# First pair's products in five steps inside the modulation, token loads and stores moved to GpSimd's queue, zeroing of result rows over 16 rows

## The chip, the cores and the metric

The kernel runs on one core of one Trainium2 chip. The metric is the device time of one execution in microseconds (us), and a kernel's time is the median over its runs. The engines are TensorE (PE; its weight loads are PEld), VectorE (DVE), ScalarE (ACT) and GpSimd (POOL). SyncE (SP) computes nothing and issues transfers; SPq, ACTq and POOLq stand for the instruction streams that issue transfers.

## The reference

A two-layer diffusion backbone works on 1024 latent tokens and 256 context tokens of width 1024. Layer 0 is neighbourhood attention with 16 heads and a hierarchical mixture of experts, layer 1 a bidirectional recurrent block and another mixture of experts. All layers are modulated by rows made from the condition vectors:

```python
m = silu(cond) @ ada_w[l] + ada_b[l]       # 6 * 1024 values, for c and for c_ctx
h = rmsnorm(x, norm_g[l, 0]) * (1 + scale) + shift
qkv = h @ w_qkv + b_qkv                    # one pair of heads: 128 columns each of q, k, v
s = softmax(q k^T / 8 + bias)              # window of 8 x 16 positions and all context keys
x = x + gate * ((s v) @ w_o + b_o)
y = sum over 2 chosen experts of weight * (silu(h w1[e]) * (h w3[e])) @ w2[e]
```

The first three lines are the modulation stage here; attention follows. The experts write their result rows to a buffer in DRAM, which must be zero where no expert writes, so that a later gather reads zeros.

## The kernel before, in words

**modulation** (L170 to L458) is one block of five instruction streams. The two condition vectors are multiplied by `ada_w`, 50.3 MB in all. It is read in NG = 6 groups g of 2048 columns, each in KD = 8 tiles k of 128 x 2048 (1 MB), so 48 tiles in 8 buffers. For each tile TensorE does four products of 512 columns ("ada product", L431). The profile counts each as two passes, so one tile is x8. At a group's end DVE adds the bias `ab` and writes `mo[g % 2]` (L388, four adds), and ACT stores `mo` to `mod_d` (L311) and loads the bias rows of group g + 2 (L269). A tile may be loaded again once the group before has used its buffer (`a_used`, L219).

Group 0 holds shift and scale for the first norm. After it TensorE spreads them over 128 partitions (L445), DVE makes `g_rows` (L393) and ACT `sh_rows` (L300). From then on the ten token tiles n (128 tokens each, eight of `x` and two of `ctx`) are prepared beside the groups:

- load into `xt[n % 4]` by SP (L208). From n = 4 on SP waits in its queue until tile n - 4 is normed (`h_ok`, L207)
- sum of squares on DVE (`squares`, L326), square root on ACT (`root_`, L259), then reciprocal, scale and shift on DVE (`norm`, L334 to L340) into `hb[n % 3]`
- eight transposes on TensorE (L456) into PSUM, and copy to `hT` by ACT (`evac`, L263).

`WITH` says which tiles are normed after which group: 0, 1, 2 after group 0; 3, 4, 5 after group 1; 6, 7 after group 2; 8, 9 after group 3. Their transposes stand at the start of the next group. ACT's stream is strictly in order: pieces of the group, the wait for `m_ready`, bias loads, store, the `evac`s, the `root_`s.

Two token tiles make a chunk c of 256 tokens. `FIRST` places the q, k and v products of the first pair of heads for each chunk (`piece`, L406 and L271) behind ada products: V at (g, k), K at (g, k + 1), T (two transposes of V) and Q at (g, k + 2), with the five places (2,0), (3,0), (3,3), (4,0), (5,0). V, K and Q are eight matmuls of 256 columns each (x16 in the profile, L420), T is L413. `LOAD_X` and `LOAD_SLAB` say behind which ada tile SP loads tokens and the three weight slabs.

**attention** (L505 to L778) starts when every stream of modulation has ended. Per pair h of 8, TensorE does the scores, transposes and outputs of pair h and between them the products of pair h + 1 (L726), V first. SP loads the slabs of pair h + 1 (L550) and the bias tables (L555), and zeroes an eighth of the result rows, 592 rows of 4 KB, in one transfer (`clear_slots`, L558 to L562). The source is `zero`, and the rows are laid out over 74 partitions, 8 rows from each. In SP's queue the first of these transfers stands in front of the slabs of pair 1. The block ends only when all eight have landed (L570).

```python
        load_pair(0, first=True)
        sp.wait_ge(zr_ok, 1)
        clear_slots(0)
        with sp.Fori(1, PAIRS) as h:
            load_pair(h)
            clear_slots(h)
        sp.wait_ge(cl_ok, 16 * PAIRS)
```

Everything after attention (projection, experts, combine, recurrent layer) is untouched.

Of the kernel before, what the change touches and what calls it, by code (L numbers as in the profile page):

```python
# [11 lines left out]
ACT = mybir.ActivationFunctionType  # L12
# [74 lines left out]
def program(nc, A, out):  # L87
    root = ExitStack()
    with root:
# [51 lines left out]
        def by_columns(rows_ap, n):  # L141
# [28 lines left out]
        def modulation(hT, first, room):  # L170
            slab, qT, kT, VT, V, bq, mask, sl_in, w_ps, w_used = first
            with ExitStack() as st:
# [14 lines left out]
                ss, rt = sbuf(st, "ss_b", [P, 2]), sbuf(st, "rt_b", [P, 2])  # L187
                c_in, c_th, c_si, a_ch = sem("c_in"), sem("c_th"), sem("c_si"), sem("a_ch")
                ab_in, bq_in, bq_ok = [sem(f"ab_in{j}") for j in range(2)], sem("bq_in"), sem("bq_ok")
                w_in = [sem(f"ada_in{k}") for k in range(KD)]  # L190
                a_used = sem("ada_used")
                m_ready, m_out = sem("mod_ready"), [sem(f"mod_out{j}") for j in range(2)]
                k_id, k_done, k_io, k_cst = sem("k_id"), sem("k_done"), sem("k_io"), sem("k_cst")
                ng_in, rows_ps, gain_ok, sh_ok = sem("b_ng"), sem("b_rows"), sem("b_gain"), sem("b_shift")
                x_in = [sem(f"b_x{j}") for j in range(NXB)]
# [5 lines left out]
                with nc.Block() as block:  # L201
                    @block.sync
                    def _(sp):
                        def load_x(n):
                            src = by_columns(A["x"][0], n) if n < NTL else A["ctx"][0, (n - NTL) * P:(n - NTL + 1) * P, :]
                            if n >= NXB:
                                sp.wait_ge(h_ok, n - NXB + 1)  # L207
                            sp.dma_start(xt[n % NXB][:, :], src).then_inc(x_in[n % NXB], 16)  # L208
# [4 lines left out]
                        for n in range(FRONT):  # L213
                            load_x(n)
# [11 lines left out]
                        sp.wait_ge(bq_in, 16)  # L226
# [24 lines left out]

                    @block.scalar
                    def _(a):
                        def root_(n):
                            j = n % 2
                            a.wait_ge(sum_ok, n + 1)
                            if n >= 2:
                                a.wait_ge(dv, 2 * (n - 2) + 1)
                            a.activation(rt[:, j:j + 1], ss[:, j:j + 1], ACT.Sqrt, bias=epst[:, :]).then_inc(sqrt_ok, 1)  # L259
# [5 lines left out]

                        def load_bias(g):
                            for j in range(QT):
                                for r in range(2):
                                    a.dma_start(ab[32 * j + r:32 * j + r + 1, g % 2, :], abv[j, :, g]).then_inc(ab_in[g % 2], 16)  # L269
# [16 lines left out]
                        load_bias(0)  # L286
                        load_bias(1)
# [8 lines left out]
                        for g in range(NG):  # L296
                            if g == 0:
                                for w, part, b0 in ROWS_PS[1::2]:
                                    a.wait_ge(rows_ps, 2 * w + 2)
                                    a.activation(sh_rows[:, w, :], banks(b0, 2), ACT.Copy).then_inc(sh_ok, 1)  # L300
                            for i, (pg, k, what, c) in enumerate(FIRST):
                                if pg == g:
                                    piece(i, what, c)
                            for n in WITH.get(g - 1, ()):
                                if n in LATE:
                                    root_(n)
                            a.wait_ge(m_ready, QT * (g + 1))
                            if g + 2 < NG:
                                load_bias(g + 2)
                            for j in range(QT):  # L310
                                a.dma_start(mod_d[:, g * GC + j * CW4:g * GC + (j + 1) * CW4],  # L311
                                            mo[g % 2][32 * j:32 * j + 2, :]).then_inc(m_out[g % 2], 16)
                            for n in WITH.get(g - 1, ()):
                                evac(n)
                            for n in WITH.get(g, ()):
                                if n not in LATE:
                                    root_(n)
                        for b in range(2):
                            a.wait_ge(m_out[b], 16 * QT * NG // 2)

                    @block.vector
                    def _(v):
                        def squares(n):
                            j = n % 2
                            v.wait_ge(x_in[n % NXB], 16 * (n // NXB) + 16)
                            v.tensor_tensor_reduce(junk, xt[n % NXB][:, :], xt[n % NXB][:, :], 1.0 / D, 0.0, ALU.mult, ALU.add,  # L326
                                                   ss[:, j:j + 1]).then_inc(sum_ok, 1)
                            v.wait_ge(sum_ok, n + 1)

                        def norm(n, w):  # L330
                            j, b = n % 2, n % NHB
                            link = Chain(v, dv, 2, n)
                            v.wait_ge(sqrt_ok, n + 1)
                            link(v.reciprocal(ss[:, j:j + 1], rt[:, j:j + 1]))  # L334
                            if n >= NHB:
                                v.wait_ge(tr_ok, n - NHB + 1)
                            link(v.scalar_tensor_tensor(out=hb[b][:, :], in0=xt[n % NXB][:, :], scalar=ss[:, j:j + 1],
# [40 lines left out]
                        for n in range(3):  # L378
                            once(v.tensor_copy(tile(1, n), expand(rowp[:, :], (2, GC_))))
                            once(v.tensor_tensor(tile(0, n), tile(1, n), expand(colp[:, n * GC_:(n + 1) * GC_], (1, GR)), ALU.max))  # L380
                        for g in range(NG):
                            v.wait_ge(a_used, KD * (g + 1))
                            v.wait_ge(ab_in[g % 2], 16 * 2 * QT * (g // 2 + 1))
# [12 lines left out]
                            tiles = WITH.get(g, ())  # L396
                            for n in tiles:
                                if n == tiles[0] or n in LATE:
                                    squares(n)
                                if n != tiles[-1] and n + 1 not in LATE:  # L400
                                    squares(n + 1)
                                norm(n, 0 if n < NTL else 1)

                    @block.tensor
                    def _(t):
# [17 lines left out]

                        t.wait_ge(c_si, 1)
                        for g in range(NG):
                            if g >= 2:
                                t.wait_ge(m_ready, QT * (g - 1))
                            for k in range(KD):
# [19 lines left out]
                            for n in WITH.get(g - 1, ()):  # L448
                                t.wait_ge(h_ok, n + 1)
                                if n >= 2:  # L450
                                    t.wait_ge(ev_ok, n - 1)
                                else:
                                    t.wait_ge(sh_ok, 2)
                                    t.wait_ge(gain_ok, 2)
                                for k in range(KD):
# [1398 lines left out]
```

## Time and profile before

| what | value |
|---|---|
| time, median of 3 runs | 3108.96 us (3108.54 to 3112.82) |
| the profiled execution's own time | 3110.24 us |
| span of its trace | 3108.4 us |
| granted clock of TensorE, mean | 0.921 of full speed |
| modulation block | 0 to 198.6 us |
| attention block | 198.6 to 925.8 us |
| busy PE / DVE / ACT / POOL | 85% / 35% / 30% / 13% |

The profiled execution lies 1.84 us outside of its span and 1.28 us above the median. A timeline row gives the start, the duration, the engine, the line of the kernel, the operation, output and inputs, the number of instructions merged, and in brackets the idle time before with what ended it. The clock is the share of full speed that was granted to TensorE.

### The profile page before, as it was taken

Reading aid. Unit: us, or ns where it says so; the run is one execution under the profiler, and the core shown is the slowest. Engines: PE = TensorE matmul, PEld = TensorE weight load, DVE = VectorE, ACT = ScalarE, POOL = GpSimd, SP = SyncE. Lnnn points to the kernel's source line nnn. Section 1 sums busy time; section 2 is a strip of 40 time slices with the busy share of each in tenths; the row PEclk is TensorE's granted clock in tenths of the full one; section 3 lists DMA queues with packets and bytes.
Section 4 is the critical chain, followed back from the end, with each engine's and each line's share of the span. In section 5 each row is a group of like instructions: output and inputs, shape, how many; then the busy total and the mean of one; then the engine's idle time right before and its main releaser. Section 6 shows DMA issues by size and latency. Waiting matters only on the chain. (4 is left out here: it accounts for less than half of the span.)

```text
span 3108.4 us, 68456 instructions
## 1 busy us (share of the span) xinstructions
PE 2628.8 (85%) x27112; PEld 1751.6 (56%) x27113; DVE 1092.4 (35%) x2328; ACT 927.1 (30%) x2036; POOL 389.8 (13%) x574
## 2 busy tenths in 40 slices
PE   5857999999978959999999359999959599999980
PEld 1536777777754536666666224544425466666650
DVE  3312333333343342222222564556444322222226
ACT  1113444344440003333333223334310033333332
POOL 0000000000001102222222310000011022222223
PEclk8878999999998979999999669999979699999995
DMA  9832111111105347999999550010042589999986
GB/s 352 301 120 74 58 46 46 51 40 58 44 26 160 102 192 300 416 411 406 417 417 417 209 150 27 27 40 27 0 165 88 216 354 413 405 417 417 418 343 225
DMA packets 157785, 652.37 MB, mean 210 GB/s; under 512 B 41600, under 2 KB 55936, under 8 KB 102368
## 3 DMA queue, kind: packets, MB, share of 16 engines
q1 hardware_dynamic: 126512, 547.79, 45.3%
q10 hardware_dynamic: 15600, 55.79, 4.6%
q0 software_dynamic: 15552, 47.20, 4.2%
q8 instruction: 73, 1.20, 0.2%
q14 instruction: 48, 0.39, 0.0%
HBM read 575.65 MB, written 75.07 MB: 209 GB/s over the span
## 5 line engine op out<-in xcount | busy, mean ns | idle before, releaser
L1155 PE MATMUL PS<-wt,xT 128*32 128x256 f32 x13056 | 753.2, 381 | 56.4 <-issue 28.3
L1155 PEld LDWEIGHTS PS<-wt,xT 128*32 128x32 f32 x13056 | 505.2, 110 | 274.4 <-issue 80.3
L726 PE MATMUL PS<-hT,slab 128*128 128x256 f32 x1680 | 386.1, 383 | 39.0 <-DMA slab<-in_qkv_s 38.5
L1095 ACT ACTIVATE y<-PS 32x256 f32<-32x256 f32 x832 | 311.6, 375 | 304.1 <-PE PS L1170 295.3
L1170 PE MATMUL PS<-wt,hidT 128*32 128x256 f32 x6528 | 396.1, 380 | 3.5 <-ACT y L1095 3.5
L726 PEld LDWEIGHTS PS<-hT,slab 128*128 128x128 f32 x1680 | 312.7, 191 | 84.6 <-DMA slab<-in_qkv_s 38.9
L1308 DVE STREAM_TRANSPOSE xT<-xg 128x256 f32<-128x256 f32 x210 | 93.5, 445 | 706.8 <-PE PS L1155 686.5
L1170 PEld LDWEIGHTS PS<-wt,hidT 128*32 128x32 f32 x6528 | 256.6, 110 | 100.9 <-issue 5.6
L1060 POOL DMA_INDIRECT xg<-h_d,ib x216 | 211.3, 978 | 174.8 <-POOL ib L1057 174.8
L1089 ACT ACTIVATE th<-PS 128x128 f32<-128x128 f32 x210 | 58.3, 277 | 526.2 <-PE PS L1155 521.0
L661 DVE TENSOR_REDUCE low<-PS 128x1 f32<-128x256 f32 x160 | 66.2, 422 | 415.1 <-PE PS L707 344.0
L1750 PE MATMUL PS<-uT,wg 128*128 128x512 f32 (+1 forms) x384 | 148.0, 545 | 20.5 <-ACT tr L1577 20.5
L933 PE MATMUL PS<-wo,OT 128*128 128x512 f32 x320 | 143.9, 609 | 17.7 <-DMA wr<-in_moe_w_expert 9.2
L1739 PE MATMUL PS<-hT,wu 128*128 128x512 f32 (+1 forms) x384 | 140.0, 526 | 8.1 <-DMA wu<-in_lru_w_in 8.1
L1057 POOL COPY ib<-idx 128x1 int32 (+1 forms) x216 | 39.3, 182 | 850.0 <-DVE xT L1308 707.1
L835 POOL TENSOR_TENSOR xt_p<-xt_p,bg 128x1024 f32<-128x1024 f32 x18 | 42.1, 2343 | 827.2 <-DVE bg L850 658.9
L933 PE MATMUL PS<-wo,zT 128*128 128x512 f32 x256 | 115.3, 610 | 35.2 <-DMA wo<-in_lru_w_o 29.1
L629 ACT ACTIVATE probT<-PS 128x640 f32<-128x640 f32 (+2 forms) x160 | 98.7, 617 | 110.0 <-PE PS L736 108.4
L1750 PEld LDWEIGHTS PS<-uT,wg 128*128 128x128 f32 x384 | 75.7, 198 | 94.9 <-issue 70.2
L736 PE MATMUL PS<-ident,prob 128*128 128x128 f32 x672 | 106.7, 284 | 21.6 <-issue 10.2
L1320 DVE STREAM_TRANSPOSE hidT<-hid 128x128 f32<-128x128 f32 x208 | 64.8, 312 | 169.8 <-PE PS L1170 168.7
L620 ACT ACTIVATE prob<-PS,low 128x640 f32<-128x640 f32 (+2 forms) x160 | 112.9, 708 | 25.0 <-DVE low L670 23.1
(248 smaller groups left out, 2588.1 us busy)
## 6 DMA issues: line engine op xcount, KB each, us to landing
wt<-in_w SPq DMA_DIRECT2D x256, 1024.0 KB, 22.8
wt<-in_w2s SPq DMA_DIRECT2D x128, 1024.0 KB, 23.2
OT<-in_ada_w SPq DMA_DIRECT2D x30, 1024.0 KB, 18.6
ys_d<-y ACTq DMA_DIRECT2D x52, 512.0 KB, 7.8
ys_d<-zero SPq DMA_DIRECT2D x8, 2368.0 KB
aw<-in_ada_w SPq DMA_DIRECT2D x18, 1024.0 KB, 23.1
slab<-in_qkv_s SPq DMA_DIRECT2D x24, 512.0 KB, 3.8
x_d<-x_p ACTq DMA_DIRECT2D x18, 512.0 KB, 3.4
```

What stands on the lines that cost most here:

```text
L620: a.activation(prob[j][:, 0:n], SF[:, o:o + n], ACT.Exp, bias=bias, scale=-1.0, accum_out=sums[:, j:j + 1]).then_inc(ex_ok, 1)
L629: a.activation(probT[j][:, 0:n], PT[:, 0:n], ACT.Copy).then_inc(pe_ok, 1)
L726: mm = pe.matmul(W, slab[m][:, k, :], hT[:, k, c * PIECE:(c + 1) * PIECE], start=(k == 0), stop=(k == KD - 1))
L736: mm = pe.transpose(PT[:, c * P:(c + 1) * P], prob[j][:, c * P:(c + 1) * P], ident[:, :])
L933: mm = t.matmul(PS[:, 2 * (n % 2) + h, :], Z[:, k, n * P:(n + 1) * P], wo[:, k, h * 512:(h + 1) * 512], start=(k == 0), stop=(k == KD - 1))
L1060: g.indirect_dma_start(out=xg[j][:, :], out_offset=None, in_=h2v, in_offset=bass.IndirectOffsetOnAxis(ap=ib[j][:, :], axis=0)).then_inc(g_ ...
L1095: ins = a.activation(buf[STRIP * j:STRIP * (j + 1), g * QD:(g + 1) * QD], PS[32 * g:32 * g + 32, DOWN, 0:QD], ACT.Copy)
L1155: mm = t.matmul(PS[32 * g:32 * g + 32, UP, 0:QD], xT[:, k * 32:k * 32 + 32], wt[b][:, q, c * 1024 + g * QD:c * 1024 + g * QD + QD], start= ...
L1170: mm = t.matmul(PS[32 * g:32 * g + 32, DOWN, 0:QD], hT[:, k * 32:k * 32 + 32], wt[b][:, q, c * 1024 + g * QD:c * 1024 + g * QD + QD], star ...
L1308: v.transpose(xT[:, :], xg[j][:, :]).then_inc(xT_ok, 1)
L1739: mm = t.matmul(dst[:, c:c + wd], w[:, k, o * P:(o + 1) * P], hT[:, k, c:c + wd], start=(k == 0), stop=(k == KD - 1))
L1750: mm = t.matmul(dst[:, c:c + wd], wg[:, q, k, o * P:(o + 1) * P], uT[k][:, c:c + wd], start=(k == 0), stop=(k == 1))
```

## The change

The transposes of chunk c now stand behind one ada product of their own (`STEPS`: (1,4), (2,3), (3,2), (4,1), (5,0)), and the chunk's V, K, T and Q behind the next three, so a step comes every seven tiles. `AFTER` says which chunks DVE norms after which group. The sums and roots have ten columns instead of two, tiles 0 and 1 have their squares taken before group 0 is done, and ACT takes the roots of tiles n + 2 ahead of the copies of n. SP loads only tokens 0 to 3; tokens 4 to 9, all bias rows (one transfer for both rows instead of two) and the stores of `mo` are issued by GpSimd. `clear_slots` uses 16 partitions with 37 rows from each, and slot 0 is cleared last.

```diff
-        WITH, LATE = {0: (0, 1, 2), 1: (3, 4, 5), 2: (6, 7), 3: (8, 9)}, (4, 5)
-        NHB, NXB, FRONT = 3, 4, 3
-        LOAD_X = {(1, 0): 3, (2, 3): 4, (2, 4): 5, (2, 6): 6, (2, 7): 7, (3, 5): 8, (3, 7): 9}
-        LOAD_SLAB = {(1, 2): 2, (1, 4): 1, (1, 6): 0}
-        FIRST = [(g, k + i, what, c) for c, (g, k) in enumerate(((2, 0), (3, 0), (3, 3), (4, 0), (5, 0)))
-                 for what, i in (("V", 0), ("K", 1), ("T", 2), ("Q", 2))]
+        AFTER = {0: (0, 1), 1: (2,), 2: (3,), 3: (4,)}
+        STEPS = ((1, 4), (2, 3), (3, 2), (4, 1), (5, 0))
+        FIRST = [(g, k + i, what, c) for c, (g, k) in enumerate(STEPS)
+                 for what, i in (("V", 1), ("K", 2), ("T", 3), ("Q", 3))]
+        NHB, NXB = 3, 4
+        LOAD_X, LOAD_SLAB = {(1, 0): 2, (1, 1): 3}, {(1, 2): 2, (1, 3): 1, (1, 4): 0}
...
-                        for n in range(FRONT):
-                            load_x(n)
+                        load_x(0)
+                        load_x(1)
...
+                        def load_bias(n):
+                            for j in range(QT):
+                                row = abv[j, 0, n, :]
+                                both = bass.AP(tensor=row.tensor, offset=row.offset, ap=[[0, 2], [1, CW4]])
+                                g.dma_start(ab[32 * j:32 * j + 2, n % 2, :], both).then_inc(ab_in[n % 2], 16)
+
+                        def store(n):
+                            g.wait_ge(m_ready, QT * (n + 1))
+                            for j in range(QT):
+                                g.dma_start(mod_d[:, n * GC + j * CW4:n * GC + (j + 1) * CW4],
+                                            mo[n % 2][32 * j:32 * j + 2, :]).then_inc(m_out[n % 2], 16)
+
+                        def load_x(n):
+                            src = by_columns(A["x"][0], n) if n < NTL else A["ctx"][0, (n - NTL) * P:(n - NTL + 1) * P, :]
+                            g.wait_ge(h_ok, n - NXB + 1)
+                            g.dma_start(xt[n % NXB][:, :], src).then_inc(x_in2[n % NXB], 16)
+
+                        load_bias(0)
+                        load_bias(1)
+                        for n in range(NG):
+                            store(n)
+                            if n + 2 < NG:
+                                load_bias(n + 2)
+                            for c in AFTER.get(n, ()):
+                                for x in (2 * c + NXB, 2 * c + NXB + 1):
+                                    if x < NT:
+                                        load_x(x)
+                        for b in range(2):
+                            g.wait_ge(m_out[b], 16 * QT * NG // 2)
...
+                        root_(0)
+                        root_(1)
+                        for w, part, b0 in ROWS_PS[1::2]:
+                            a.wait_ge(rows_ps, 2 * w + 2)
+                            a.activation(sh_rows[:, w, :], banks(b0, 2), ACT.Copy).then_inc(sh_ok, 1)
+                        for c in range(NT // 2):
+                            for n in (2 * c, 2 * c + 1):
+                                if n + 2 < NT:
+                                    root_(n + 2)
+                            for n in (2 * c, 2 * c + 1):
+                                evac(n)
+                            for i, (_, _, what, pc) in enumerate(FIRST):
+                                if pc == c:
                                     piece(i, what, c)
...
+                        squares(0)
+                        squares(1)
                         for g in range(NG):
...
-                            tiles = WITH.get(g, ())
-                            for n in tiles:
-                                if n == tiles[0] or n in LATE:
-                                    squares(n)
-                                if n != tiles[-1] and n + 1 not in LATE:
-                                    squares(n + 1)
-                                norm(n, 0 if n < NTL else 1)
+                            for c in AFTER.get(g, ()):
+                                for n in (2 * c, 2 * c + 1):
+                                    if c:
+                                        squares(n)
+                                for n in (2 * c, 2 * c + 1):
+                                    norm(n, 0 if n < NTL else 1)
...
+                                if (g, k) in STEPS:
+                                    for n in range(2):
+                                        turn(2 * STEPS.index((g, k)) + n)
...
-                            n, rows = SLOTS // PAIRS, 74
+                            n, rows = SLOTS // PAIRS, 16
                             dst = ys_d[bass.ds(h * n, n), :].rearrange("(i p) d -> p i d", p=rows)
                             sp.dma_start(dst, expand(zero[0:rows, :], (1, n // rows))).then_inc(cl_ok, 16)
 
                         load_pair(0, first=True)
                         sp.wait_ge(zr_ok, 1)
-                        clear_slots(0)
                         with sp.Fori(1, PAIRS) as h:
                             load_pair(h)
                             clear_slots(h)
+                        clear_slots(0)
                         sp.wait_ge(cl_ok, 16 * PAIRS)
```

`turn(n)` is the former loop of eight transposes with its waits, made a function.

## Rows read from the trace of the kernel before

**Rows 1.** Costliest groups on the page: the products of the next pairs on PE
```profile
L726 PE MATMUL PS<-hT,slab 128*128 128x256 f32 x1680 | 386.1, 383 | 39.0 <-DMA slab<-in_qkv_s 38.5
```
**Rows 2.** Busy time of stretches of early attention; the first row names the columns
```profile
core 0: us, PE busy (x) PEld busy (x) DVE busy (x) ACT busy (x) POOL busy (x), PEclk, DMA share, GB/s
...
210.90:249.40 38.50, 0.00 (x0) 0.00 (x1) 2.63 (x9) 2.25 (x5) 0.00 (x0) 0.50 0.27 97
249.40:292.00 42.60, 42.60 (x268) 33.92 (x270) 13.44 (x40) 17.02 (x37) 3.86 (x4) 0.95 0.13 54
```
**Rows 3.** Timeline of early attention: SP's issues, and PE on both sides of its gap
```profile
199.57 0.34 SPq L562 DMA_DIRECT2D ys_d<-zero  x1
...
200.82 36.68 SPq L550 DMA_DIRECT2D slab<-in_qkv_s  x3
...
209.74 1.12 PE L736 MATMUL PS<-ident,prob 128*128 128x128 f32 x4
...
249.40 5.75 PE L726 MATMUL PS<-hT,slab 128*128 128x256 f32 x16 [38.54 <-DMA slab<-in_qkv_s]
```
**Rows 4.** DMA: rate over 0 to 250 us in 6.25 us slices; issues from 198 to 212
```profile
GB/s 108 261 399 422 420 324 420 414 417 417 357 266 325 246 263 424 415 415 419 274 287 275 218 48 275 270 421 121 0 3 69 51 52 52 53 53 230 140 50 53
...
ys_d<-zero SPq DMA_DIRECT2D x1, 2368.0 KB
slab<-in_qkv_s SPq DMA_DIRECT2D x1, 512.0 KB, 48.5
```
**Rows 5.** What SP's queue waited for from 62 to 93 us: total, times, longest
```profile
SPq L208 <- DVE hb_b L340: 13.4, 2, 12.9
SPq L220 <- PE PS L431: 12.9, 6, 4.5
```
**Rows 6.** Timeline: PE's ada products at tiles (0,0), (1,0) to (1,3), and (1,7)
```profile
16.76 1.89 PE L431 MATMUL PS<-OT,csil 128*2 128x512 f32 x8 [16.76 <-DMA OT<-in_ada_w]
...
44.20 5.84 PE L431 MATMUL PS<-OT,csil 128*2 128x512 f32 x32
...
61.57 1.89 PE L431 MATMUL PS<-aw,csil 128*2 128x512 f32 x8 [1.85 <-DMA aw<-in_ada_w]
```
**Rows 7.** Timeline of group 4: transposes, squares, copies to hT, pieces V, K, Q, ada products
```profile
137.98 1.97 PE L456 MATMUL PS<-ident,hb_b 128*128 128x128 f32 x16
...
142.25 1.22 DVE L326 CUSTOM_DVE_ANT_0 gt_rows<-xt_b 128x1024 f32<-128x1024 f32 x1
...
144.68 1.94 ACT L263 ACTIVATE hT<-PS 128x1024 f32<-128x1024 f32 x2 [7.95 <-issue]
...
146.76 5.85 PE L420 MATMUL PS<-hT,slab 128*128 128x256 f32 x16 [5.85 <-ACT hT L263]
...
153.52 3.72 PE L420 MATMUL PS<-hT,slab 128*128 128x256 f32 x16
...
158.41 3.62 PE L420 MATMUL PS<-hT,slab 128*128 128x256 f32 x16
...
163.68 2.76 PE L431 MATMUL PS<-aw,csil 128*2 128x512 f32 x24
```
**Rows 8.** Timeline: end of modulation
```profile
193.10 2.84 DVE L388 TENSOR_TENSOR mo<-PS,ab 2x512 f32<-2x512 f32 x4 [23.75 <-PE PS L431]
195.97 1.16 ACTq L311 DMA_DIRECT2D mod_d<-mo  x4
...
198.59 0.96 POOL L574 MEMSET zero<- 128x1024 f32 x1 [195.19 <-POOLq L201]
```
**Rows 9.** Transfers issued by GpSimd: one in the first expert stage; the gathers, us to landing
```profile
1160.05 0.98 POOL L1060 DMA_INDIRECT xg<-h_d,ib  x1 [0.83 <-POOL ib L1057]
...
y_c<-ys_d,ib_c POOLq DMA_INDIRECT x36, 6.5
```
**Rows 10.** Timeline: last zeroing transfer, last computing instruction of attention
```profile
793.23 0.28 SPq L562 DMA_DIRECT2D ys_d<-zero  x1
...
925.30 0.28 ACT L638 ACTIVATE OT<-PS 128x128 f32<-128x128 f32 x1 [0.84 <-PE PS L759]
```

More of the change, by code:

```diff
@@ L186, in modulation @@
                 hb = [sbuf(st, f"hb_b{j}", [P, D]) for j in range(NHB)]
[L187 removed]
+                ss, rt = sbuf(st, "ss_b", [P, NT]), sbuf(st, "rt_b", [P, NT])
                 c_in, c_th, c_si, a_ch = sem("c_in"), sem("c_th"), sem("c_si"), sem("a_ch")
[L189 removed]
+                ab_in, bq_in, bq_ok = [gather_sem(f"ab_in{j}") for j in range(2)], sem("bq_in"), sem("bq_ok")
                 w_in = [sem(f"ada_in{k}") for k in range(KD)]
                 a_used = sem("ada_used")
[L192 removed]
+                m_ready, m_out = sem("mod_ready"), [gather_sem(f"mod_out{j}") for j in range(2)]
                 k_id, k_done, k_io, k_cst = sem("k_id"), sem("k_done"), sem("k_io"), sem("k_cst")
                 ng_in, rows_ps, gain_ok, sh_ok = sem("b_ng"), sem("b_rows"), sem("b_gain"), sem("b_shift")
[L195 removed]
+                x_in, x_in2 = [sem(f"b_x{j}") for j in range(NXB)], [gather_sem(f"b_more{j}") for j in range(NXB)]
                 sum_ok, sqrt_ok, h_ok, tr_ok, ev_ok = sem("b_sum"), sem("b_sqrt"), sem("b_h"), sem("b_tr"), sem("b_ev")
@@ L254, in root_ @@
                         def root_(n):
-                            j = n % 2
                             a.wait_ge(sum_ok, n + 1)
-                            if n >= 2:
-                                a.wait_ge(dv, 2 * (n - 2) + 1)
-                            a.activation(rt[:, j:j + 1], ss[:, j:j + 1], ACT.Sqrt, bias=epst[:, :]).then_inc(sqrt_ok, 1)
+                            a.activation(rt[:, n:n + 1], ss[:, n:n + 1], ACT.Sqrt, bias=epst[:, :]).then_inc(sqrt_ok, 1)
                         def evac(n):
@@ L295, in _ @@
                         a.wait_ge(k_id, 3)
[L296 to L302, printed above, removed]
-                                    piece(i, what, c)
[L304 to L319, printed above, removed]
+                        root_(0)
[11 more added lines that the diff above has]
+                                if pc == c:
+                                    piece(i, what, c)
                     @block.vector
@@ L422, in piece, with turn @@
                             mm.then_inc(w_ps, 1)
+                        def turn(n):
+                            t.wait_ge(h_ok, n + 1)
+                            if n >= 2:
+                                t.wait_ge(ev_ok, n - 1)
+                            else:
+                                t.wait_ge(sh_ok, 2)
+                                t.wait_ge(gain_ok, 2)
+                            for k in range(KD):
+                                mm = t.transpose(banks(2 + 2 * (n % 2), 2)[:, k * P:(k + 1) * P],
+                                                 hb[n % NHB][:, k * P:(k + 1) * P], ident[:, :])
+                            mm.then_inc(tr_ok, 1)
                         t.wait_ge(c_si, 1)
@@ L447, in _ @@
                                     mm.then_inc(rows_ps, 1)
[L448 to L455, printed above, removed]
-                                    mm = t.transpose(banks(2 + 2 * (n % 2), 2)[:, k * P:(k + 1) * P],
-                                                     hb[n % NHB][:, k * P:(k + 1) * P], ident[:, :])
-                                mm.then_inc(tr_ok, 1)
         def load_rows(eng, s, l, sub, ng_row, tmp_ng):
```

29 lines of the change are left out of this document (11 added, 18 removed).

## The prediction, made before the changed kernel was run

> **What bounds the kernel now.** I read the costliest groups first and looked for idle time of TensorE, the busiest engine. One row stands out: the products of the next head pair sat idle 39.0 us, of which 38.5 wait for a weight slab [rows 1]. The stretches say that this is one hole: from 210.9 to 249.4 PE does nothing at a clock of 0.50, and behind it PE is busy all of the time [rows 2]. So a gap closed in early attention should be gained in full.
>
> The timeline gives the cause. SP issued the zeroing of slot 0 at 199.57 and the slabs only then, its three slab issues stretching over 36.68 us; PE stopped after 209.74 + 1.12 = 210.86 and went on at 249.40 [rows 3]. While the zeroing ran the core moved 51 to 53 GB/s, where loads over 128 partitions ran at 415 to 422; the first slab took 48.5 us to land [rows 4]. 53/420 is an eighth, two engines of 16: 2.42 MB / 53 = 45.7 us, so the zeroing ended at about 246 and the slab's share behind it on those two a little later. The part of the Trainium skill on this (DMA: Bandwidth & Descriptors, "Why a DMA increments its semaphore by 16 and not by 1") says that a DMA uses the largest number up to 16 that divides the slowest dimension of both sides; that makes 2 of 74, as the rate shows, and 16 of 16.
>
> The second place is modulation, 198.6 us. Its DMA runs at 420 GB/s up to 62 us, then at 246 to 357 in four of the next five slices, and falls again after 119 [rows 4]. SP's queue shows why in the first of these: it stood 12.9 us at one token load that waits for a norm, with ada tiles queued behind [rows 5]. Near the middle PE works, but each group has a hole: in group 4 the V piece waited 5.85 us for the copies to `hT`, because ACT does the store of `mo` first, and then ran at 5.85 instead of 3.72 us, at the lower clock [rows 7].
>
> **The slab wait.** Clearing slot 0 goes behind everything, so slab V of pair 1 is the first large transfer of attention. It is issued at about the place of the old zeroing, 12.3 us after the block's start PE wants it, and three slabs are 1.57 MB, 3.7 us at 420. It has landed long before. Removed: 249.40 - 210.86 = 38.5 us. The first piece behind the gap was cold (5.75 us [rows 3]) and will be, since PE is cold in the first 12 us anyway; nothing for that. Bounds: 36, if another operand is late next (bias tables, whose loads are behind the slabs), and 40, if the clock rises sooner. I take 38.5.
>
> **Zeroing on 16 partitions.** Seven transfers come one per pair, behind that pair's slabs, and two at the end. No row has a transfer of 16 partitions. Between the full rate (2.42 MB / 420 = 5.8 us) and that of 74 partitions (45.7) the time is the same: the last issue was at 793.23, attention ended at 925.6 [rows 10], 132 us for two transfers of at most 45.7. Cost 0 at either; PE's work hides it.
>
> **Modulation, up to the first step.** Two instead of three token tiles stand ahead of `ada_w`: 0.52 MB / 420 = 1.25 us, so tile (0,0) lands at 15.5 instead of 16.76, and group 1 starts on PE at 42.95 instead of 44.20 [rows 6]. Bias loads leave ACT for GpSimd, hidden behind the tiles of group 0. Before, tile (1,7) was there at 61.57 [rows 6]. SP's list up to it holds as many bytes as before with those two tiles counted, but GpSimd may issue tokens 4 to 7 from about 46 us on, as norms end, which share the 16 engines: up to 4 x 1.25 = 5 us, so it lands between 61.6 and 66.6. Chunk 0 runs in the same time: transposes at about 53, then V (cold, 5.85), K and Q. That ends near 72, no longer at the start of group 2 behind all copies and stores. Four ada products later, at 75 to 80, step 1 begins; I take 76. PE's queue had the same transposes at 63 but its products from 74 to 88.
>
> **Modulation, step by step.** From step 1 on all seven tiles of a step cost, warm: two transposes 1.97; product and V 0.9 + 3.65; product and K the same; product, T and Q 1.2 + 3.65 (153.52 + 3.72 to 158.41 is 1.2); four more products at 2.76/3 = 0.92, 3.7 [rows 7]. Sum 19.6, and 0.4 for the end of the second copy: 20 us. DMA needs 7 x 2.5 = 17.5, plus 2.5 for two tokens in one step, so PE sets the pace and no tile is late. Steps 1 to 4 and the rest: 4 x 20 = 80 us.
>
> New waits: `root_(n + 2)` stands ahead of the copies on ACT, and its sum comes after the group's adds on DVE. Step 2 is at (3,2): from the end of (2,7) it takes adds 2.84, two sums 2.6, a root 0.3, two copies 1.94 [rows 7, 8], with handovers 8.1 us, while PE has 3 products, the transposes and one product, 5.5: late by 2.6. Step 3 at (4,1) has one product less: 3.5. Steps 1 and 4 have room or no roots. After such a pause V may be cold, as in [rows 7]: 2 us each. Together 10 us (bounds 0 and 12). PE then ends at 76 + 80 + 10 = 166 (158 to 176).
>
> **The end of the block.** Before: adds from 193.10 to 195.94, attention's first instruction at 198.59 [rows 8], 2.65 later. GpSimd now issues the four stores. The only rows of its issues are gathers, 0.98 each and 0.83 idle between [rows 9], against 1.16 us for ACT's four. Four are 3.9 to 7.2, so 2.8 to 6.0 more, below by 0 if small ones are cheap; I take 2.8, as the stores compute no indices. End: 166 + 0.1 + 2.84 + 2.65 + 2.8 = 174.4, that is 24.2 less than 198.6. Ends: 158 + 5.6 = 163.6 (35 gained) and 176 + 5.6 + 6 = 187.6 (11).
>
> **Sum.** 38.5 + 24.2 = 62.7 us; from the profiled 3110.24 this gives 3047.5, from the median, 1.28 lower, 3046.3. All behind attention moves forward unchanged. Nothing within 0.2% (6.2 us) can be told from no change here.
>
> **Rivals.**
> - *Modulation gains almost nothing* (0 to 11 us). The work of SP's queue waits in POOL's instead; every step waits for DVE or ACT, and PE falls cold each time (5 steps x 5 us are the 25). For it: the roots ahead of the copies. Against it: only two steps have less room than the chain needs. Time 3108.96 - 38.5 - 6 = 3065 (3059 to 3071). In the Trainium skill (Trainium Kernel Development and Optimization, "Key Constraints") DMAs of all three queues share the same engines, and using several of them only saves issue time. By that the token loads gain nothing, and the time is this rival's. But SP's 12.9 us [rows 5] are a wait inside the queue, no issue time. Chance 0.13.
> - *The stalls don't come* and modulation follows its transfers: over 35 us gained, 3034 or less. Against it the DVE chain above. Chance 0.05.
> - *The 16 rows go over fewer engines.* Two change nothing. One would make 91 us of each: issued at 793.23, the last two would end at 976, 50 us after attention's old end of 925.6 [rows 10], and slabs queued behind would wait some 2 us per pair, 12 together: 3046 + 62 = 3108, no change. Below 37 GB/s it begins to cost. The quotient 53/420 for 74 speaks for a rule of divisors, so against it. Chance 0.02.
> - *GpSimd's queue becomes the bound* (slower). After the adds of group 0 at 38.6 it has 24 stores, 16 bias loads and 6 token loads, 46 in a strict order, and DVE waits for bias and stores of two groups earlier. At t us each the block ends at 38.6 + 46 t + 2: 0.98 [rows 9] gives nothing, and it decides from 2.9 us on, where it passes 174. Slower than before, 38.5 us being gained in attention, needs t over 4.3. If each transfer waited for the one before to land, 6.5 us as the gathers take [rows 9], the block would end at 340: 3109 + 141 - 38.5 = 3212. Against it: gathers follow each other at 1.8 us, not 6.5. Chance 0.03.
>
> **How the numbers follow.** Forecast 0.75 (3036 to 3059), rivals 0.13, 0.05, 0.02, 0.03; 0.02 for what I don't see. The bounds of the terms give 3108.96 - 36 - 11 = 3062 and 3108.96 - 40 - 35 = 3034; they hold the forecast's case and a third of the first rival, about 0.8. Faster by over 0.2%: 0.95; within: 0.02; slower: 0.03.
>
> **What would show it.** No wait of PE for a slab in early attention, and in the 50 us after its start full-rate slices, then slices of zeroing at a high rate, not at 53. Modulation ends at 174 (164 to 188). SP waits only for ada buffers. PE's V pieces of steps 2 and 3 wait 2 to 4 us for ACT's copies, the others under 1. Four POOL issues of about 1 us follow the last adds. I am wrong if the gap before L726 merely moves to another operand, if the steps are further apart than 24 us, or if stages behind attention change in length.

## The result and the profile after

The changed kernel takes 3093.45 us (3090.72 to 3098.35, 5 runs) against 3110.51 for the kernel before in the same comparison: a ratio of 0.9947 with the interval 0.9932 to 0.9961. It is 17 us faster where 62.7 were predicted, and lies outside the predicted range. Its profiled execution has a span of 3089.5 us, 18.9 less than before. By blocks:

| block | before | after | change | predicted |
|---|---|---|---|---|
| modulation | 198.6 | 183.6 | -15.0 | -24.2 |
| attention | 727.2 | 719.1 | -8.1 | -38.5 |
| all behind it | 2182.6 | 2186.8 | +4.2 | 0 |

Each kernel has one trace, and blocks with the same code differ from trace to trace. Modulation as before takes 192.5 to 198.6 us (the kernel before and runs 3 and 4), the changed one 181.8 to 186.2 us (the changed kernel and runs 1, 2 and 5 to 8). So the gain there is 15.0 us in this pair of traces, and 6 to 17 us if other pairs are taken. One source of the spread is the clock of single V pieces: the last one took 6.54 us in the kernel before and 3.69 in runs 3 and 4.

From the changed kernel's page, the row that answers to [rows 1] and two others that grew:

```profile
L741 PE MATMUL PS<-hT,slab 128*128 128x256 f32 x1680 | 387.9, 384 | 0.5
...
L751 PE MATMUL PS<-ident,prob 128*128 128x128 f32 x672 | 106.9, 285 | 47.6 <-ACT probT L644 28.2
...
L644 ACT ACTIVATE probT<-PS 128x640 f32<-128x640 f32 (+2 forms) x160 | 98.7, 617 | 139.5 <-PE PS L751 97.0
```

The slab wait is gone, idle 39.0 before and 0.5 now. In its place TensorE waits 28.2 us for `probT`, a plain copy on ScalarE. Three stretches of the changed kernel: attention's start, what was the hole, and a place inside attention.

```profile
core 0: us, PE busy (x) PEld busy (x) DVE busy (x) ACT busy (x) POOL busy (x), PEclk, DMA share, GB/s
183.59:195.60 12.01, 6.47 (x25) 4.09 (x26) 3.58 (x12) 3.44 (x6) 7.92 (x9) 0.50 0.89 234
195.60:238.20 42.60, 42.60 (x288) 34.16 (x288) 16.31 (x49) 19.99 (x43) 0.74 (x1) 0.99 0.45 49
371.80:391.30 19.50, 3.54 (x12) 1.90 (x12) 2.29 (x7) 0.00 (x0) 3.85 (x4) 0.56 0.97 140
```

PE works through where it stood still [rows 2]. But at 371.8 all compute engines stop for most of 19.5 us, ACT wholly, while the 16 DMA engines are busy for 0.97 of the time and move only 140 GB/s. The timeline of this place:

```profile
370.82 0.38 ACT L620 ACTIVATE V<-PS 128x256 f32<-128x256 f32 x1
371.75 0.35 SPq L577 DMA_DIRECT2D ys_d<-zero  x1
376.15 1.11 PE L751 MATMUL PS<-ident,prob 128*128 128x128 f32 x4 [5.46 <-issue]
391.32 0.60 ACT L644 ACTIVATE probT<-PS 128x512 f32<-128x512 f32 x1 [20.12 <-issue]
392.06 1.09 PE L751 MATMUL PS<-ident,prob 128*128 128x128 f32 x4 [12.36 <-ACT probT L644]
```

This is where the loop over pairs jumps back, after pair 1. ACT's input was ready at 377.26, its instruction ran at 391.32, and what ended its wait is no semaphore ("issue"). The same happens after pair 3 (20.8 us). The third end of the loop body leads out of the loop, and nothing happens there. The two pairs with such a jump take 110.4 and 109.8 us between slab issues, before 94.9 and 95.4: 30 us, the whole loss in attention.

Modulation in the changed kernel's timeline, with the last tile before the first step, the transposes of step 1, the V pieces of steps 2 and 3, and the transposes of step 4:

```profile
62.20 1.89 PE L454 MATMUL PS<-OT,csil 128*2 128x512 f32 x8 [7.58 <-DMA OT<-in_ada_w]
...
86.44 1.97 PE L443 MATMUL PS<-ident,hb_b 128*128 128x128 f32 x16
...
111.48 3.69 PE L430 MATMUL PS<-hT,slab 128*128 128x256 f32 x16 [1.54 <-ACT hT L287]
...
134.16 5.38 PE L430 MATMUL PS<-hT,slab 128*128 128x256 f32 x16 [3.16 <-ACT hT L287]
...
152.44 1.97 PE L443 MATMUL PS<-ident,hb_b 128*128 128x128 f32 x16
```

And its end, which answers to [rows 8]:

```profile
172.37 2.84 DVE L399 TENSOR_TENSOR mo<-PS,ab 2x512 f32<-2x512 f32 x4 [17.82 <-PE PS L454]
175.50 2.05 POOL L258 DMA_DIRECT2D mod_d<-mo  x4 [18.61 <-DVE mo L399]
...
183.59 0.96 POOL L589 MEMSET zero<- 128x1024 f32 x1 [6.04 <-POOLq L201]
```

### The profile page after: what moved, and what is told of

It reads as the page before. It is cut to its first block and busy times, and to the rows that moved or that the text cites. A ratio compares the mean times of both kernels' runs of the same rounds, so it can differ in the third digit from the quotient of the medians.

```text
span 3089.5 us, 68426 instructions
## 1 busy us (share of the span) xinstructions
PE 2621.9 (85%) x27112; PEld 1748.2 (57%) x27113; DVE 1092.2 (35%) x2328; ACT 927.2 (30%) x2036; POOL 419.4 (14%) x628
## 5 line engine op out<-in xcount | busy, mean ns | idle before, releaser
L1170 PE MATMUL PS<-wt,xT 128*32 128x256 f32 x13056 | 754.6, 382 | 57.7 <-issue 27.4
L948 PE MATMUL PS<-wo,OT 128*128 128x512 f32 x320 | 142.2, 603 | 20.0 <-DMA wr<-in_moe_w_expert 11.5
L1072 POOL COPY ib<-idx 128x1 int32 (+1 forms) x216 | 39.3, 182 | 852.5 <-DVE xT L1323 708.6
L751 PE MATMUL PS<-ident,prob 128*128 128x128 f32 x672 | 106.9, 285 | 47.6 <-ACT probT L644 28.2
L1765 PEld LDWEIGHTS PS<-uT,wg 128*128 128x128 f32 x384 | 76.0, 199 | 94.9 <-issue 70.2
L751 PEld LDWEIGHTS PS<-ident,prob 128*128 128x128 f32 x672 | 76.6, 143 | 93.4 <-issue 78.1
## 6 DMA issues: line engine op xcount, KB each, us to landing
ys_d<-zero SPq DMA_DIRECT2D x8, 2368.0 KB, 25.7
```

The costliest lines, as they stand in the source:

```text
L751: mm = pe.transpose(PT[:, c * P:(c + 1) * P], prob[j][:, c * P:(c + 1) * P], ident[:, :])
L948: mm = t.matmul(PS[:, 2 * (n % 2) + h, :], Z[:, k, n * P:(n + 1) * P], wo[:, k, h * 512:(h + 1) * 512], start=(k == 0), stop=(k == KD - 1))
L1170: mm = t.matmul(PS[32 * g:32 * g + 32, UP, 0:QD], xT[:, k * 32:k * 32 + 32], wt[b][:, q, c * 1024 + g * QD:c * 1024 + g * QD + QD], start= ...
L1765: mm = t.matmul(dst[:, c:c + wd], wg[:, q, k, o * P:(o + 1) * P], uT[k][:, c:c + wd], start=(k == 0), stop=(k == 1))
```

## The experiments

The experiments are medians of 4 runs, the first two rows of 5; the ratio is to the kernel before on the same chip, whose medians were 3112.1 (the first four), 3108.85 (the next four) and 3110.2 (the last four). The last two columns are from the profiled executions: the blocks' lengths, and the idle time of ACT before its first copy at a jump (the longer of the two).

| kernel | us | ratio | modulation, attention | gap |
|---|---|---|---|---|
| before | 3110.5 | 1 | 198.6, 727.2 | 5.8 |
| changed | 3093.5 | 0.9947 | 183.6, 719.1 | 20.8 |
| 1: 74 partitions | 3066.1 | 0.9851 [0.9835, 0.9868] | 183.9, 690.3 | 9.5 |
| 2: 128 partitions | 3068.2 | 0.9854 [0.9837, 0.9870] | 186.2, 692.2 | 9.6 |
| 3: before, 16 partitions | 3092.5 | 0.9928 [0.9912, 0.9945] | 194.9, 709.6 | 5.9 |
| 4: before, slot 0 last | 3074.1 | 0.9878 [0.9862, 0.9895] | 192.5, 687.9 | 5.9 |
| 5: ACT unrolled | 3063.5 | 0.9847 [0.9827, 0.9867] | 181.8, 686.2 | 6.1 |
| 6: zeroing mid pair | 3056.5 | 0.9824 [0.9808, 0.9841] | 183.7, 685.4 | 6.8 |
| 7: 72 idle instructions | 3065.3 | 0.9851 [0.9833, 0.9869] | 183.8, 689.6 | 6.0 |
| 8: every 8th partition | 3076.8 | 0.9891 [0.9874, 0.9907] | 183.2, 701.4 | 13.5 |
| 9: 6 + slabs later | 3057.9 | 0.9832 [0.9816, 0.9849] | 180.8, 685.5 | |
| 10: 6 + last store on SP | 3053.8 | 0.9819 [0.9802, 0.9835] | 174.5, 684.1 | |
| 11: 6 + roots after | 3053.3 | 0.9812 [0.9796, 0.9829] | 176.0, 687.2 | |
| 12: 6, 9, 10, 11 and 2 | 3048.7 | 0.9796 [0.9779, 0.9812] | 171.8, 684.7 | |

### Width or order

**1, the changed kernel with 74 partitions.**

```diff
-                            n, rows = SLOTS // PAIRS, 16
+                            n, rows = SLOTS // PAIRS, 74
```

> The changed kernel with the zeroing back on 74 partitions, slot 0 still last. Theory A: the two 20 us gaps of ScalarE in attention, at the turns of its loop over pairs, come from the zeroing, which holds all 16 DMA engines busy for 25.6 us at about 105 GB/s, with something that ScalarE needs from them behind it (its instructions). With 14 engines free again the gaps shrink to the 5.8 us of before: attention 719.1 - 30 = 689 us, the kernel 3093.5 - 30 = 3063 us. Theory B: the gaps come from the new order of the queue (slabs first, slot 0 last) or from what moved to GpSimd; then they stay, and the time is 3093 within 3 us. Either way no wait for slab V of pair 1, and modulation stays at 183.6 us.

3066.1 us: 27.4 less than the changed kernel. Theory A holds, order and GpSimd are out. The gap falls to 9.5, though, and not to 5.8 us. ACT's waits here:

```profile
ACT probT L644 <- issue: 18.8, 2, 9.5
```

**2, 128 partitions.** Seven transfers of 5 x 128 rows and one of 2 x 128.

```diff
-                            n, rows = SLOTS // PAIRS, 16
-                            dst = ys_d[bass.ds(h * n, n), :].rearrange("(i p) d -> p i d", p=rows)
-                            sp.dma_start(dst, expand(zero[0:rows, :], (1, n // rows))).then_inc(cl_ok, 16)
+                            dst = ys_d[bass.ds((h - 1) * 5 * P, m * P), :].rearrange("(i p) d -> p i d", p=P)
+                            sp.dma_start(dst, expand(zero[:, :], (1, m))).then_inc(cl_ok, 16)
```

> The changed kernel with the zeroing on all 128 partitions, seven transfers of 5 x 128 rows and a last one of 2 x 128. Theory A (what counts is how long the engines are held): at the full rate of 418 GB/s a transfer of 2.62 MB takes 6.3 us instead of 25.6, ScalarE's gaps fall to 6 to 9 us, kernel 3063 to 3068 us. Theory A2 (what counts is that all 16 engines are taken at all, and the held time is queue order): gaps stay well over 9 us. Theory B (order or GpSimd): gaps stay at 20 us, 3093 us.

3068.2 us, as run 1 within their spread. All 16 engines are taken here too, but briefly; the first row below is how a transfer landed (KB, us), the second ACT's wait.

```profile
ys_d<-zero SPq DMA_DIRECT2D x7, 2560.0 KB, 10.5
...
ACT probT L643 <- issue: 19.0, 2, 9.6
```

In the changed kernel the smaller transfer took 25.7 us, in run 8 (16 partitions, spread) 14.2. The gap follows this time: 20.8, 13.5, 9.6.

**3 and 4, one part of the edit alone on the kernel before.**

```diff
-                            n, rows = SLOTS // PAIRS, 74
+                            n, rows = SLOTS // PAIRS, 16
```

> The kernel before with 16 partitions instead of 74 and nothing else, slot 0 still ahead of the slabs. Theory A: the wait for slab V falls from 38.5 to about 38.5 - (45.7 - 25.6) = 18 us, and the two gaps of about 20 us appear at the loop turns, 15 us each more than before: 3110.5 - 20 + 30 = 3120 us. Theory B (order or GpSimd makes the gaps): no gaps, 3110.5 - 20 = 3090 us. My prediction had the width cost nothing anywhere: 3090 us too.

3092.5 us, where my theory expected 3120. The slab wait shrank to 16.0 us (18 foreseen; first row), 22.5 less than before, and attention by 17.6; where the other 4.9 went stays open. But ACT has no long gap at the jump (second row), though the zeroing is as slow as in the changed kernel.

```profile
PE PS L726 <- DMA slab<-in_qkv_s: 16.0, 1, 16.0
...
407.79 0.60 ACT L629 ACTIVATE probT<-PS 128x512 f32<-128x512 f32 x1 [5.95 <-PE PS L736]
```

```diff
-                        clear_slots(0)
                         with sp.Fori(1, PAIRS) as h:
                             load_pair(h)
                             clear_slots(h)
+                        clear_slots(0)
```

> The kernel before with slot 0 zeroed last and nothing else (74 partitions, modulation as before). Theory A: 3110.5 - 38.5 = 3072 us, no gap over 6 us of ScalarE at the loop turns, modulation 198.6 us. Theory B in the form that the order makes the gaps: 3072 + 30 = 3102 us.

3074.1 us, 38.0 less than before. The slab wait is gone and attention is 39.3 us shorter, so the step of the prediction on this wait holds. That the whole kernel gains just 38.0 is in part luck: in its trace modulation is 6.1 us shorter and all behind attention 7.0 us longer, with the code unchanged, and the interval of the ratio is 5 us wide on either side.

By run 3 a slow zeroing was not enough for the stall. It needed something that the changed modulation had brought as well. ACT's attention code itself is the same; its place is not: 72 transfer instructions in front of it were gone (48 bias loads and 24 stores), with some waits.

### What ScalarE waits for

I take the DMA queues named "instruction" to carry the engines' code. A packet of queue 8 is 16 KB (73 packets and 1.20 MB in the whole kernel); the trace doesn't say for which engine it is. At the jump of the changed kernel, three stretches in order (373 to 374 us, 375 to 388, 389 to 390; packets, MB, share of 16 engines):

```profile
q1 hardware_dynamic: 197, 0.28, 97.2%
q8 instruction: 1, 0.02, 7.1%
...
q1 hardware_dynamic: 350, 1.39, 96.5%
...
q1 hardware_dynamic: 23, 0.09, 88.2%
q8 instruction: 1, 0.02, 6.8%
```

One such packet arrives at 373, PE goes on at 376.15. Then only zeroing moves, 350 packets in 13 us. The next packet of code comes at 389, and ACT goes on at 391.32. In run 1, with two engines zeroing, that second packet is moved at 375 to 376 and ACT resumes at 379.29; in run 3, the kernel before with slow zeroing, it comes only at 420, but ACT has run since 407.79, so it had the code that it needed. Runs 8 and 2, between the two, fit as well: the second packet is moved at 381 and 380, and ACT goes on at 382.89 and 381.59. Read so, the changed kernel's loop starts where the jump needs one block of code more before ACT can go on. Three runs test that.

**5, ScalarE's loop written out.**

```diff
-                        turns(a, pair)
+                        for h in range(PAIRS):
+                            pair(h, h % 2, h == PAIRS - 1)
```

> The changed kernel (16 partitions) with ScalarE's attention stream written out for all eight pairs instead of a loop over two; all other engines as they are. Theory A (ScalarE's gap is the fetch of its next block of instructions, asked for at the backward jump and stuck behind the zeroing): without the jump ScalarE reads ahead and the two gaps of 20 us go to what TensorE's own turn leaves, under 6 us: 3093 - 30 = 3063 us. Rival C (ScalarE waits for a semaphore or for data that the zeroing holds up, such as a table or a slab): the gaps stay at 20 us, 3093 us.

3063.5 us. The zeroing still takes 25.8 us per transfer; ACT, which no longer jumps, waits for PE alone:

```profile
375.52 0.60 ACT L644 ACTIVATE probT<-PS 128x512 f32<-128x512 f32 x1 [6.07 <-PE PS L752]
```

A semaphore or late data would have held it here too. Rival C falls.

**6, the zeroing in the middle of a pair.**

```diff
                                     sp.sem_inc(sp_passed, 1)
+                                    if m == 1:
+                                        clear_slots(h)
...
                             load_pair(h)
-                            clear_slots(h)
```

> The changed kernel with the same transfers over 16 partitions, issued between the slab loads of V and K of each pair, some 15 to 20 us into it, instead of at its end where the loops turn. Theory A: nothing is fetched at a jump then, ScalarE's gaps fall to the 9.4 us that 74 partitions leave: 3066 us within 4. Rival C: the transfers are as long and hold the same queue, the slabs of K and Q even more, so stalls of similar size: 3090 us or more.

3056.5 us, 9.5 under the expectation. The transfer is issued at 343.17 and has landed when the loops turn:

```profile
343.17 0.35 SPq L579 DMA_DIRECT2D ys_d<-zero  x1
...
376.80 0.60 ACT L645 ACTIVATE probT<-PS 128x512 f32<-128x512 f32 x1 [6.42 <-PE PS L752]
```

Without any zeroing at the jump the two gaps are 6.4 and 6.8 us and not 9.4 and 9.5 as in run 1, so even the transfer on 74 partitions had cost some 3 us at each.

**7, 72 instructions that do nothing.** `pad` is a semaphore that nobody waits for.

```diff
+                        for _ in range(72):
+                            a.sem_inc(pad, 1)
                         a.sem_inc(w_used, 1)
```

> The changed kernel with 72 idle semaphore increments at the head of ScalarE's stream, as many as the transfers it issued before the change. They cost ScalarE time only where it is idle. Theory A with position (the kernel before with 16 partitions had no gap over 6 us since its loop lay otherwise in the 16 KB blocks of instructions): the gaps of 20 us go, 3063 us within 4. Theory A without position: gaps of 20 us stay, 3093 us, and why the kernel before was spared is open.

3065.3 us: more instructions at the head of a stream, and the kernel is 28 us faster. The zeroing is as slow as before (25.7 us), at the same place in the pair, and the gap is that of the kernel before. A packet of queue 8 comes only at 389 here too, but ACT has run since 377.18:

```profile
377.18 0.60 ACT L646 ACTIVATE probT<-PS 128x512 f32<-128x512 f32 x1 [6.00 <-PE PS L753]
```

**8, 16 partitions, but every eighth.**

```diff
-                            sp.dma_start(dst, expand(zero[0:rows, :], (1, n // rows))).then_inc(cl_ok, 16)
+                            sp.dma_start(dst, expand(zero[0:P:P // rows, :], (1, n // rows))).then_inc(cl_ok, 16)
```

> The changed kernel with the 16 source partitions 0, 8, 16, ... 120 instead of 0 to 15. Theory D (16 neighbouring partitions share few ports of the on-chip memory, hence 105 instead of 418 GB/s): a transfer of 2.42 MB takes 6 to 8 us instead of 25.6, ScalarE's gaps fall to 9 or 10 us, 3066 us within 4. Rival E (a single partition per DMA engine is slow by itself): 25 us as before, gaps of 20 us, 3093 us.

Between the two theories: landing 14.2 us instead of 25.7, gap 13.5, 3076.8 us.

```profile
ys_d<-zero SPq DMA_DIRECT2D x8, 2368.0 KB, 14.2
...
ACT probT L644 <- issue: 26.6, 2, 13.5
```

Spreading the 16 partitions takes 11.5 of the 25.7 us away, 128 partitions take 15.2 (with a little more data). So most of the excess over run 2 goes with the partitions being neighbours. The rest goes with reading one partition per engine, or with the 37 descriptors of an engine coming from one source row; this was not separated.

### Modulation

**9, slabs of pair 0 behind later tiles.**

```diff
-        LOAD_X, LOAD_SLAB = {(1, 0): 2, (1, 1): 3}, {(1, 2): 2, (1, 3): 1, (1, 4): 0}
+        LOAD_X, LOAD_SLAB = {(1, 0): 2, (1, 1): 3}, {(1, 4): 2, (1, 5): 1, (1, 6): 0}
```

> On top of the run with the zeroing in mid pair (3056.5 us): the three slab loads of modulation stand behind tiles (1,4), (1,5), (1,6) instead of (1,2), (1,3), (1,4). Theory F (the first step began at 64 us and not at 53 because tile (1,4) landed only at 62.2, with two slabs and three token tiles in front): the tile lands 2.5 to 3 us sooner, the first step and all after it with it, modulation 183.7 - 2.5 = 181 us, kernel 3054. Rival: the step is set by something else (a norm, a later tile); no change, 3056.5.

3057.9 us, no change. The first step did start 7 us sooner (62.67 in run 6), but step 1 came when it came before (85.19 in run 6):

```profile
55.82 3.67 PE L443 MATMUL PS<-ident,hb_b 128*128 128x128 f32 x16
...
85.31 1.97 PE L443 MATMUL PS<-ident,hb_b 128*128 128x128 f32 x16
```

So up to step 1 PE follows the arrival of tiles, wherever the slabs stand in the queue. The block is 2.9 us shorter because its V piece in step 3 took 3.69 us at a granted clock of 1.00 and not 6.71 at 0.54 as in run 6; the wait in front of it was 3.15 us in both.

**10, the last store on SP's queue.** GpSimd leaves out group 5.

```diff
+                        sp.wait_ge(m_ready, QT * NG)
+                        for j in range(QT):
+                            sp.dma_start(mod_d[:, n * GC + j * CW4:n * GC + (j + 1) * CW4],
+                                         mo[n % 2][32 * j:32 * j + 2, :]).then_inc(m_last, 16)
+                        sp.wait_ge(m_last, 16 * QT)
```

> On top of the run with the zeroing in mid pair: the last group's four stores are issued by SP, idle by then, and not by GpSimd. Theory G (on GpSimd's queue they cost 8.4 us from the last adds to attention's first instruction, on ScalarE's before 2.65): 5 to 6 us less, modulation 178 us, kernel 3051. Rival: the 8.4 us are the barrier between blocks; no change, 3056.5.

3053.8 us. From the adds' end at 171.93 to attention's start it is 2.6 us, as it had been on ACT's queue:

```profile
171.96 1.19 SPq L227 DMA_DIRECT2D mod_d<-mo  x4
174.52 0.96 POOL L597 MEMSET zero<- 128x1024 f32 x1 [20.91 <-POOLq L201]
```

Behind the same adds GpSimd's queue had cost 8.4 us, 5.8 more: 2.05 for the issues and 6.04 behind them. Most of the 6.04 is not the landing. The last four stores landed 1.6 us after their issue, the last bytes by 178.2, and attention started at 183.59. From the changed kernel, 175 to 184 us:

```profile
mod_d<-mo POOLq DMA_DIRECT2D x4, 4.0 KB, 1.6
```

What fills the other 5.4 us no run separates; it goes when the stores leave GpSimd's queue. The block is 9.2 us shorter than in run 6, and 3.0 of the other 3.4 are step 3's V piece, which took 3.69 us here. The medians differ by 2.7 and their runs overlap (3049.5 to 3056.6 against 3056.2 to 3058.3); the block's gain is shown by the profile.

**11, the roots behind the copies.**

```diff
                             for n in (2 * c, 2 * c + 1):
-                                if n + 2 < NT:
+                                if not c:
                                     root_(n + 2)
                             for n in (2 * c, 2 * c + 1):
                                 evac(n)
+                            for n in (2 * c, 2 * c + 1):
+                                if c and n + 2 < NT:
+                                    root_(n + 2)
```

> On top of the run with the zeroing in mid pair: ScalarE takes the roots of tiles 4 to 9 behind the two copies of its step instead of ahead of them. Theory H (the copies of steps 2 and 3 wait for roots of tiles that nobody needs yet: 1.5 and 3.2 us of TensorE idle, and one V piece at the low clock, 1.7 us): modulation 6 us shorter, 178 us, kernel 3051. Rival: the later roots make a norm late in its turn and give it back; 0 to 2 us.

3053.3 us, modulation 7.7 shorter than in run 6. The V pieces of steps 2 and 3:

```profile
108.47 3.69 PE L433 MATMUL PS<-hT,slab 128*128 128x256 f32 x16 [0.28 <-ACT hT L287]
...
128.27 3.69 PE L433 MATMUL PS<-hT,slab 128*128 128x256 f32 x16 [0.28 <-ACT hT L287]
```

Both waits are down to 0.28 us (1.52 and 3.15 in run 6), no piece is cold, and the steps follow at 20.1, 19.8 and 19.8 us. The waits are 4.1 us of the gain. The cold piece of run 6 is 3.0 more, but runs 9 and 10 had none there either, with the waits in place.

**12, the three edits with the zeroing in mid pair and on 128 partitions.**

> The three edits together with the zeroing in mid pair and over 128 partitions. If they add up (2.5 + 5.5 + 6) modulation ends at 170 us; the width costs nothing in mid pair, gaps as with 16 there. Kernel 3056.5 - 14 = 3042 us. If the steps become bound by transfers instead, only half of the 8.5 us of the first and third edit come: 3047.

3048.7 us (3045.2 to 3051.8), the best: 44.8 faster than the changed kernel, but 6.7 over the 3042 that the sum of the parts gave. Modulation ends at 171.8, 11.9 sooner than in run 6 (14 said), and attention is as long as there. The stages behind it took 5.8 us more than in run 6, with the same code.

## Why the prediction was wrong

**The slab wait: right.** 38.5 us were counted, attention is 39.3 us shorter in run 4, and the changed kernel has no such wait. The first piece there took 4.15 us, between the 5.75 of before, which was forecast again, and the 3.62 to 3.72 of a warm one.

**The zeroing on 16 partitions: the step that failed.** It was costed at "0 at either; PE's work hides it", because the transfers need not land before attention's end. It costs 27.4 us (run 1). Its length was within the bounds: 25.7 us lies between 5.8 and 45.7. Wrong was to look only for who waits for its end. This transfer is on all 16 DMA engines (share 0.97) and delays what others fetch through them, the engines' own code as I read it: the second packet of queue 8 came 16 us after the first. [rows 4] had the clue that I read for the slab only: a share of an eighth of the engines leaves seven eighths free. By the Trainium skill (DMA: Bandwidth & Descriptors, "Queues, rings and completion order") a DMA engine changes between its queues only at packet ends and drains a packet of some 9 to 17 descriptors first. Each engine had 37 rows of 4 KB; if a row is a descriptor, one took 25.7/37 = 0.69 us, and the estimate by that page is 6 to 12 us for a turn. The trace shows 16 us between the two packets, more than the estimate. When the second was asked for isn't seen, and how the queues take turns was not tested. The same page's rule that the prediction cites, two engines for 74 and all for 16, agrees with the shares, 0.13 and 0.97.

That the same transfer stalls ACT in the changed kernel and not in runs 3 and 7 is a matter of what stands in front of its loop. That this means a block of code more or less is the reading that fits the packets; no run shows the blocks themselves. The trace of before couldn't show it.

**Modulation: mechanism right, two terms mis-sized.** Tile (0,0) at 15.17 (said: 15.5) and group 1 at 42.98 (42.95) are as worked out. Step 1 began at 86.4 instead of 76: tile (1,4), taken to be there at about 53, was used at 62.2, since two slabs and tokens 2 to 6 were in front or beside it. I had counted the tokens' 5 us for tile (1,7) and left the first step in its place. Step 1 is set by the tiles too: in run 9 it came as late though the first step was sooner. The price of 1.25 us per token also took the full rate, and the rate was not full. While the tokens were on their way, from 50 to 62 us, the core moved this much:

```profile
DMA packets 708, 3.35 MB, mean 279 GB/s; under 512 B 69, under 2 KB 69, under 8 KB 529
```

From 33 to 42 us it was 275 GB/s. At 420 the same bytes would have come 4.0 and 3.1 us sooner (an estimate from these rates). Which of the loads is the slow one was not tested.

From the start of step 1 to PE's end it took 85.9 us, said 90: waits of 1.54 and 3.16 us where 2.6 and 3.5 were foreseen, one cold V piece (5.38) instead of two. Step 3 took 24.4 us, over the 24 that was set as a sign of being wrong. The end of the block was 8.4 us behind the adds, said 5.45: the four issues are cheap (0.51 us each, not 0.98), but 6.04 us passed behind them, of which 0.6 to the last landing and 5.4 without a cause that a trace shows (run 10). Together 10.4 - 4.1 + 2.9 = 9.2, the difference between 183.6 and 174.4.

**Behind attention: +4.2 us,** forecast unchanged. Runs 4 and 12, with like code there, have 2189.5 and 2193.2 us against 2182.6 of before, which is the shortest of all fourteen traces. In run 4 it is waits for weights, 2 us each at two places, and 2.4 us more work of TensorE; in run 12 mostly the latter, 7.5 us. Whether this is chance or follows from code or timing is open.

**The rivals.** None was it. The one that had the 16 rows go over fewer engines looked at this very transfer from the wrong side. Modulation's rival with a cold PE in every step did not come about.

## What to carry over

A transfer that nobody waits for may cost time when it holds every DMA engine (27.4 us in the changed kernel, no gap at the jump in runs 3 and 7): look at the DMA share and the GB/s of its stretch together, and keep slow transfers away from places where an engine jumps back and must fetch code. A wait that ends in "issue" at the head of a loop body, with a packet of an instruction queue just before its end, may be a fetch; moving the transfer, unrolling that engine's loop or shifting its code by some instructions tells it from a data wait. One trace per kernel is not enough to tell 5 us in a block of 190: compare with other kernels that have the same code there. And when several loads are put in front of a tile, count them for the first use behind them, not for the last.

## What was not expected of the hardware

- 2.42 MB from 16 neighbouring partitions took 25.7 us on all 16 engines (94 GB/s), from every eighth partition 14.2 us (171), and 2.62 MB from 128 partitions 10.5 us (250, with the loads ahead of it in the queue). From 74 partitions two engines alone made 53 GB/s, so a single engine was over four times as fast there as in the first case.
- The packets of queue 8, read as code, are 16 KB, and ScalarE stood for 20 us until one that came late. Whether a jump stalls depends on what stands in front of the loop: 72 idle instructions there changed the kernel by 28 us.
- With the last four stores on GpSimd's queue the block's end came 5.8 us later than on SP's, though they had landed 5.4 us before it.
